# First feed forward: up and down slabs in turn, 14 of 16 down slabs by seven block products, sums on GpSimd

## The chip, the cores and the metric

One Trainium2 chip, one of its cores. The kernel is one launch that computes two transformer blocks for 256 tokens in float32. The metric is the device time of that launch in microseconds; three runs of the kernel before gave 883.88, 883.88 and 883.88, median 883.88. The profiled execution, from which all rows here come, took 884.08 with a span of 882.2.

## The reference, cut to what matters

The change touches the feed forward of the first block, with `h` 256 x 1024, `w1` 1024 x 4096 and `w2` 4096 x 1024:

```python
u = rmsnorm(h, norm_ff_g[l]) @ w1[l]
h = h + jnp.square(jax.nn.relu(u)) @ w2[l]
return rmsnorm(h, final_norm_g)
```

Before it stand the mixer and the cross attention, after it the second block, whose first weights are those of `in_w_in_2`.

## The kernel before, in words

**Slabs.** All weights stream through the core as numbered slabs of 128 partitions x 2048 float32 (1 MB). Three buffers in turn (`RING` = 3) hold the raw slab (`raw`) and its two parts: `whi`, the value rounded to fp32r, made by ScalarE's copy (`hi`, L1389), and `wlo`, the rest, made by VectorE's subtraction of two SBUF operands (`lo`, L1944). TensorE makes each product in three passes (`mm3`, L718 to L720): high by high, high by low, low by high. SyncE loads slab n when `lo` of slab n-3 is done; ScalarE splits slab n when it has landed and TensorE has finished slab n-3. Every engine has one queue in order, and the order of the work on each is written out by hand.

**An up slab** (16 of them, `w1`, 256 columns) gives two 128-row tiles of the hidden layer, transposed, by 48 matmuls of 256 columns (`t_slab`). ScalarE takes the relu from PSUM into `ru` (`relu_step`, L1695), VectorE squares it into `sq` (`square`, L2305), ScalarE rounds it into `hid_hi` (`relu_hi`, L1699), VectorE makes `hid_lo` (`square_lo`, L2319). All 32 hidden tiles are kept in SBUF.

**A down slab** (16 of them, `w2`, 256 rows) adds the product of two hidden tiles with 256 x 1024 weights to the four PSUM banks `acc`. Plainly this is 8 block products of three passes, 24 matmuls of 512 columns (`row_slab`). Six of the 16 (down slabs 1, 3, 5, 7, 9, 11) are done by the seven products of Winograd's form of Strassen's rule instead (`seven_slab`), 21 matmuls. Those need four sums of weight blocks and four of hidden blocks:

```python
link(dve.tensor_tensor(b22, b22, b12, ALU.subtract))
dve.tensor_tensor(b12, b12, b11, ALU.subtract).then_inc(sev["t"], 1)
...
link(dve.tensor_tensor(b11, b22, b11, ALU.add))
dve.tensor_tensor(b21, b21, b11, ALU.subtract).then_inc(sev["t"], 1)
```

All sums are VectorE's. The four weight sums (`forms`, 128 x 512 each) are made in place in the raw slab, then split by ScalarE (`forms_hi`, L1717) and VectorE (`forms_lo`, L2343) into the rooms of `xhi` and `xlo`, which are free once the last up slab is done. The four hidden sums (128 x 128 each) stand in `square`, three of them in room of `xn`. Such a slab is loaded by two DMAs of 512 KB, and only 1536 of its 2048 columns are split by `hi` and `lo`. Four of the seven products go to the banks `tb` and are added to `h` once, in `fold` (VectorE), after slab 11.

**Order.** All 16 up slabs run first (one by `first_slab`, which begins amid the transposes of `h`, 15 in a loop), then the 16 down slabs. The last one (`last_row_slab`) is followed by quarters of the residual (`residual`, VectorE) and their transposes. The second block begins there.

**GpSimd** has nothing in this stretch but `square_scale` and a DMA at its start, and `gain_fin` (L599) at its end.

Of the kernel before, what the change touches and what calls it, by code (L numbers as in the profile page):

```python
# [16 lines left out]
F32 = mybir.dt.float32  # L17
# [3 lines left out]
ALU = mybir.AluOpType  # L21
# [14 lines left out]
RING = 3  # L36
SLAB = 2048
# [9 lines left out]
def plan(w):  # L47
# [40 lines left out]
    cols("w1", w["w1"], 0, 16)  # L88
    rows("w2", w["w2"], 16)
# [20 lines left out]
def two_blocks(nc, w, out):  # L110
# [14 lines left out]
    SEVEN = [first["w2"] + j for j in (1, 3, 5, 7, 9, 11)]  # L125
# [5 lines left out]
    with ExitStack() as ctx:  # L131
# [63 lines left out]
        with ExitStack() as r3:  # L195
            hid_hi = sb("hid_hi", [P, FF1 // P, T], F32R, at=r3)
            hid_lo = sb("hid_lo", [P, FF1 // P, T], F32R, at=r3)
            ru = sb("ru", [P, 512], at=r3)
            sq = sb("sq", [P, 512], at=r3)
            sum_hi = sb("sum_hi", [P, len(SEVEN), 3 * P], F32R, at=r3)  # L200
            sum_lo = sb("sum_lo", [P, len(SEVEN), 3 * P], F32R, at=r3)
# [81 lines left out]
        sev = sems("sev", "t hi lo kept folded")  # L283
# [31 lines left out]
        lasts = [first["wo"] + 3, first["xo"] + 3, first["w2"] + 15, first["w3"] + 3, NS - 1]  # L315
# [3 lines left out]
        TURNED = {"h1": first["wo"] + 3, "h2": first["xo"] + 3, "x2": first["w2"] + 15}  # L319
# [116 lines left out]

        FORMS_HI, FORMS_LO = (room[:, 32:32 + SLAB].rearrange("p (s c) -> p s c", c=512) for room in (xhi_room, xlo_room))
        sums = xn[:, 0, 0:3 * P]

        def halves(t):  # L440

            return t[:, 0:4:3, :], t[:, 1:3, :]
# [11 lines left out]
        def _(sp):  # L454
            def load(n, src=None, wait=None):
# [3 lines left out]
                if n - RING in SEVEN:  # L459
                    sp.wait_ge(sev["lo"], 2 * SEVEN.index(n - RING) + 2)  # L460
# [54 lines left out]
            for n in range(RING + 1, first["w1"]):  # L515
# [17 lines left out]
        def _(pool):  # L533
# [120 lines left out]
            for m in range(1, LEVELS):  # L654
# [60 lines left out]
        def _(pe):  # L715
# [17 lines left out]
            def t_slab(n, hi, lo, bank, value=None, fresh=None):  # L733
# [4 lines left out]
                for c in range(slabs[n][3] // P):  # L738
                    o = tb[:, bank + c // 2, (c % 2) * T:(c % 2) * T + T]
# [35 lines left out]
            def seven_slab(j, hi, lo):  # L775

                n = first["w2"] + j
                i, k = SEVEN.index(n), 2 * j
                b_hi, b_lo = slab(whi, n, 2).rearrange("p k (s c) -> p (k s) c", c=512), \
                    low_slab(n, 2).rearrange("p k (s c) -> p (k s) c", c=512)  # L780
                first_one, last_one = i == 0, i == len(SEVEN) - 1

                def whole(kt, t):
                    return hi[:, kt, t * P:t * P + P], lo[:, kt, t * P:t * P + P]

                def summed(a):
# [409 lines left out]
            n0 = first["w1"] + 1  # L1196
            with pe.Fori(0, 5) as i:
                for u in range(RING):
                    pe.wait_ge(act_emptied, i * RING + (act_evacs[n0 + u] - RING))
                    t_slab(n0 + u, XHI["h2"], XLO["h2"], (u + 1) % RING, i * RING + (n0 + u + 1))  # L1200

            for j in range(15):
                pe.wait_ge(ffn["lo"], j + 1)
                if j == 1:
                    emptied(first["w1"] + 15)
                if first["w2"] + j in SEVEN:
                    seven_slab(j, hid_hi, hid_lo)
                else:
                    row_slab(first["w2"] + j, hid_hi, hid_lo, 2 * j, 32)
# [159 lines left out]
        def _(act):  # L1369
# [322 lines left out]
            def relu_step(bank, done, j, dst):  # L1692

                act.wait_ge(slab_done, done)
                act.activation(ru[:, :], tb[:, bank, :], ACT.Relu).then_inc(act_emptied, 1)  # L1695

            def relu_hi(j):
                act.wait_ge(ffn["sq"], j + 1)
                last = act.activation(hid_hi[:, 2 * j:2 * j + 2, :], sq[:, :], ACT.Copy)  # L1699
                if first["w2"] + j in SEVEN:  # L1700
                    last = act.activation(sum_hi[:, SEVEN.index(first["w2"] + j), :], sums, ACT.Copy)
                last.then_inc(ffn["hi"], 1)

            n0 = first["w1"]
            act.wait_ge(slab_done, n0 + 1)
            act.activation(ru[:, 0:T], tb[:, 0, 0:T], ACT.Relu)
            act.activation(ru[:, T:2 * T], acc[:, 1, 0, 0:T], ACT.Relu).then_inc(act_emptied, 1)
            hi(n0 + RING)
            relu_hi(0)
            def forms_hi(j):  # L1710

                n = first["w2"] + j
                i = SEVEN.index(n)
                act.wait_ge(slab_done, SEVEN[i - 1] + 1 if i else first["w2"])
                for half, (src, dst) in enumerate(zip(halves(raw_forms(n)), halves(FORMS_HI))):
                    act.wait_ge(sev["t"], 2 * i + half + 1)
                    act.activation(dst, src, ACT.Copy).then_inc(sev["hi"], 1)  # L1717

            for j in range(1, 16):
                relu_step(j % RING, n0 + j + 1, None, None)  # L1720
                if j == 15:
                    forms_hi(1)
                hi(n0 + j + RING)
                relu_hi(j)
            n0 = first["w2"]
            for j in range(14):
                if n0 + j + 2 in SEVEN:
                    forms_hi(j + 2)
                if n0 + j == SEVEN[-1]:
                    act.wait_ge(slab_done, n0 + j + 1)  # L1730
                    act.activation(ru[:, :], tb[:, 0, :], ACT.Copy).then_inc(sev["kept"], 1)
                hi(n0 + j + RING)
# [197 lines left out]
        def _(dve):  # L1930
# [372 lines left out]
            def square(j):  # L2303
                dve.wait_ge(act_emptied, act_evacs[first["w1"] + j])
                made = dve.tensor_tensor(sq[:, :], ru[:, :], ru[:, :], ALU.mult)  # L2305
                if first["w2"] + j in SEVEN:
                    link(made)
                    a11, a21, a12, a22 = (sq[:, i * P:i * P + P] for i in range(4))
                    s1, s2, s4 = (sums[:, i * P:i * P + P] for i in range(3))
                    link(dve.tensor_tensor(s1, a21, a22, ALU.add))  # L2310
                    link(dve.tensor_tensor(a21, a11, a21, ALU.subtract))
                    link(dve.tensor_tensor(s2, s1, a11, ALU.subtract))
                    made = dve.tensor_tensor(s4, a12, s2, ALU.subtract)
                made.then_inc(ffn["sq"], 1)

            def square_lo(j):
                dve.wait_ge(ffn["hi"], j + 1)
                dst, src = hid_lo[:, 2 * j:2 * j + 2, :], hid_hi[:, 2 * j:2 * j + 2, :]
                last = dve.tensor_tensor(dst, sq[:, :], src.bitcast(F32), ALU.subtract)  # L2319
# [45 lines left out]
            for j in range(16):  # L2365
                square(j)
                if j == 15:
                    forms_lo(1)
                lo(n0 + j + RING)
                square_lo(j)  # L2370
                if j == 14:
                    forms(1)
# [333 lines left out]
```

## Time and profile before

| | |
|---|---|
| median of three runs | 883.88 us |
| profiled execution | 884.08 us, span 882.2 us |
| TensorE matmuls | busy 874.6 us, 99% |
| VectorE | busy 647.6 us, 73% |
| ScalarE | busy 502.4 us, 57% |
| GpSimd | busy 117.9 us, 13% |
| granted TensorE clock | 1.0 of full speed |
| HBM read | 158.86 MB, 181 GB/s over the span |

Matmuls overlap in the pipeline, so their durations are longer than the distance from one start to the next; that distance is what a matmul costs. PE is TensorE's matmuls, DVE VectorE, ACT ScalarE, POOL GpSimd, SPq SyncE's DMA queue. A duration on DVE or POOL runs from the instruction's start in the record to its end and holds whatever it stood still in between.

### The profile page before, as it was taken

To read this page: it belongs to the slowest core of one execution; us is meant where nothing else is said; L and a number is where in the kernel's file an instruction comes from. 1 tells how busy PE (TensorE), PEld (TensorE's weight loads), DVE (VectorE), ACT (ScalarE), POOL (GpSimd) and SP (SyncE) were. 2 spreads that over 40 slices of the span, in tenths; PEclk is the share of its full clock that TensorE was granted. 3 is DMA by queue.
4 is the path that set the end of the run, shared out by engine and by line. 5 is a ranking of instruction groups with operands and counts; after the bars stand their busy time and mean duration, and the time that the engine had idled before them with its cause. 6 is when DMAs were issued, how large, how long until landed. Compare 5 with 4: busy or idle time off the path is not lost.

```text
span 882.2 us, 15673 instructions
## 1 busy us (share of the span) xinstructions
PE 874.6 (99%) x6269; PEld 809.7 (92%) x6269; DVE 647.6 (73%) x881; ACT 502.4 (57%) x741; POOL 117.9 (13%) x136
## 2 busy tenths in 40 slices
PE   9999999999999999999999999999999999999997
PEld 9998988989989999888899989999998899999886
DVE  5887987656538887998775548978686788888643
ACT  7786655546547555545473356656634766666432
POOL 5561433000001000000142250001000100000000
PEclk9999999999999999999999999999999999999999
DMA  9969444354535666466556554354556386676641
GB/s 304 319 226 311 164 144 144 104 177 148 172 94 187 195 195 197 160 230 219 191 184 210 191 191 141 104 188 138 174 191 191 105 225 195 194 198 201 192 143 48
DMA packets 137399, 160.67 MB, mean 182 GB/s; under 512 B 4161, under 2 KB 113857, under 8 KB 137089
## 3 DMA queue, kind: packets, MB, share of 16 engines
q1 hardware_dynamic: 135280, 152.83, 54.1%
q0 software_dynamic: 1344, 6.03, 2.0%
q10 hardware_dynamic: 720, 1.06, 0.3%
q8 instruction: 38, 0.62, 0.3%
q14 instruction: 17, 0.13, 0.1%
HBM read 158.86 MB, written 1.05 MB: 181 GB/s over the span
## 4 chain that ended last, share of the span: by engine, by line
PE 98%; issue 1%; ACT 0%; DVE 0%; POOL 0%; DVEq 0%; POOLq 0%; ACTq 0%
PE tb L718 18%; PE tb L719 18%; PE tb L720 18%; PE acc L718 11%; PE acc L720 11%; PE acc L719 11%; PE acc L1043 1%; PE tb L1242 0%; PE tb L1122 0%; PE acc L1272 0%; PE tb L1140 0%; PE acc L1140 0%; PE acc L1290 0%; PE acc L1122 0%; PE tb L1241 0%
## 5 line engine op out<-in xcount | busy, mean ns | idle before, releaser
L1944 DVE TENSOR_TENSOR wlo<-raw,whi 128x2048 fp32r<-128x2048 f32 (+1 forms) x138 | 313.9, 2279 | 118.5 <-ACT whi L1389 117.9
L1389 ACT ACTIVATE whi<-raw 128x2048 fp32r<-128x2048 f32 (+1 forms) x138 | 261.4, 1896 | 140.6 <-PE acc L720 85.2
L718 PE MATMUL tb<-xhi,whi 128*128 128x256 f32 x1192 | 331.8, 278 | 0.2
L719 PE MATMUL tb<-xlo,whi 128*128 128x256 f32 x1192 | 329.5, 276 | 0.0
L720 PE MATMUL tb<-xhi,wlo 128*128 128x256 f32 x1192 | 329.5, 276 | 0.0
L718 PEld LDWEIGHTS tb<-xhi,whi 128*128 128x128 f32 x1192 | 224.1, 188 | 1.1 <-issue 1.0
L719 PEld LDWEIGHTS tb<-xlo,whi 128*128 128x128 f32 x1192 | 224.2, 188 | 0.1
L720 PEld LDWEIGHTS tb<-xhi,wlo 128*128 128x128 f32 x1192 | 224.0, 188 | 0.0
L720 PE MATMUL acc<-whi,xlo 128*128 128x512 f32 x112 | 44.0, 393 | 0.0
L718 PE MATMUL acc<-whi,xhi 128*128 128x512 f32 x112 | 43.8, 392 | 0.0
L719 PE MATMUL acc<-wlo,xhi 128*128 128x512 f32 x112 | 43.8, 391 | 0.0
L1893 ACT ACTIVATE cy<-tb,cols 128x256 f32<-128x256 f32 x44 | 22.5, 561 | 32.3 <-PE tb L720 32.3
L711 POOL TENSOR_TENSOR rs<-rs,half_neg 128x1 f32<-128x1 f32 x6 | 3.3, 553 | 266.8 <-DVE rs L2563 266.8
L719 PE MATMUL acc<-wlo,vhi 128*128 128x512 f32 x88 | 34.2, 389 | 0.0
L718 PE MATMUL acc<-whi,vhi 128*128 128x512 f32 x88 | 34.2, 389 | 0.0
L720 PE MATMUL acc<-whi,vlo 128*128 128x512 f32 x88 | 34.2, 389 | 0.0
L718 PE MATMUL acc<-whi,hid_hi 128*128 128x512 f32 x86 | 33.6, 391 | 0.0
L720 PE MATMUL acc<-whi,hid_lo 128*128 128x512 f32 x86 | 33.5, 389 | 0.0
L719 PE MATMUL acc<-wlo,hid_hi 128*128 128x512 f32 x86 | 33.5, 389 | 0.0
L2619 DVE SCALAR_TENSOR_TENSOR cy<-tb,cols,cy 128x255 f32<-128x255 f32 x44 | 19.2, 478 | 14.1 <-ACT cy L1893 14.1
L718 PE MATMUL tb<-mhi,whi 128*128 128x256 f32 x96 | 27.1, 282 | 0.0
L720 PE MATMUL tb<-mhi,wlo 128*128 128x256 f32 x96 | 26.6, 277 | 0.0
(448 smaller groups left out, 1598.2 us busy)
## 6 DMA issues: line engine op xcount, KB each, us to landing
raw<-in_w_in SPq DMA_DIRECT2D x37, 1024.0 KB, 5.2
raw<-in_w SPq DMA_DIRECT2D x26, 1024.0 KB, 5.4
raw<-in_w_up SPq DMA_DIRECT2D x44, 512.0 KB, 5.0
raw<-in_w_down SPq DMA_DIRECT2D x22, 512.0 KB, 4.2
raw<-in_w_xkv SPq DMA_DIRECT2D x8, 1024.0 KB, 5.3
raw<-in_w_out SPq DMA_DIRECT2D x8, 1024.0 KB, 4.9
raw<-in_w SPq DMA_DIRECT2D x12, 512.0 KB, 4.5
raw<-in_w_mem_kv SPq DMA_DIRECT2D x4, 1024.0 KB, 5.2
```

The source lines that it names most:

```text
L711: pool.tensor_tensor(r, r, half_neg[:, 0:1], ALU.pow).then_inc(tail_rs, 1)
L718: pe.matmul(o, a_hi, b_hi, start=start, stop=False)
L719: pe.matmul(o, a_hi, b_lo, start=False, stop=False)
L720: return pe.matmul(o, a_lo, b_hi, start=False, stop=stop)
L1043: last = pe.matmul(acc[:, 1, t, i * 64:i * 64 + 64], a[:, s], lvl_view(b[:, s], m)[:, :, 1, :], start=True, stop=True)
L1389: act.activation(whi[:, n % RING, cut], raw[:, n % RING, cut], ACT.Copy).then_inc(hi_ready, 1)
L1893: last = act.activation(cy[:, b, g, :], tb[:, b, g * T:g * T + T], ACT.Identity, scale=cols[:, bass.ds(j + a, 1)], bias=cols[:, bass.ds(j ...
L1944: dve.tensor_tensor(low(n)[:, cut], raw[:, n % RING, cut], whi[:, n % RING, cut].bitcast(F32), ALU.subtract).then_inc(lo_ready, 1)
L2619: last = dve.scalar_tensor_tensor(cy[:, b, g, 1:], tb[:, b, g * T:g * T + T - 1], cols[:, bass.ds(j + c, 1)], cy[:, b, g, 1:], ALU.mult, A ...
```

## The change

The order of the slabs becomes up 0, up 1, down 0, up 2, down 1, ... up 15, down 14, down 15. Up slab j+1 lies between down slabs j-1 and j, so only three sets of hidden tiles are kept (`HIDS` = 3), and the room that this frees holds the weight sums and their parts in buffers of their own (`forms`, `forms_hi`, `forms_lo`, two each). Up products go to one bank, `acc[:, 1, 1, :]`. Down slabs 0 to 13 use the seven products; 14 and 15 are plain. All weight sums and hidden sums move from VectorE to GpSimd; the weight sums read the raw slab as it lands and write to `forms`. The four sums at the end of the seven products move to GpSimd as well, from one copy of the four `tb` banks (ScalarE, `kept`); VectorE's `fold` keeps four additions to `h`. The up loops become straight code on SyncE and TensorE.

```diff
-    cols("w1", w["w1"], 0, 16)
-    rows("w2", w["w2"], 16)
+    for kind, j in [("up", 0)] + [s for j in range(15) for s in (("up", j + 1), ("down", j))] + [("down", 15)]:
...
-    SEVEN = [first["w2"] + j for j in (1, 3, 5, 7, 9, 11)]
+    UP = [first["w1"] + max(2 * j - 1, 0) for j in range(16)]
+    DOWN = [first["w1"] + min(2 * j + 2, 31) for j in range(16)]
+    SEVEN = DOWN[:14]
...
# SyncE, load
                 if n - RING in SEVEN:
-                    sp.wait_ge(sev["lo"], 2 * SEVEN.index(n - RING) + 2)
+                    sp.wait_ge(sev["t"], 2 * SEVEN.index(n - RING) + 2)
...
# GpSimd
+            def weight_sums(j):
+                i, n = j, DOWN[j]
+                b12, b11, b21, b22 = (raw_forms(n)[:, s, :] for s in range(4))
+                t3, t1, t2, t4 = (forms[:, i % 2, s, :] for s in range(4))
+                pool.wait_ge(raw_landed[n % RING], landed[n])
+                if i >= 2:
+                    pool.wait_ge(sev["lo"], 2 * i - 2)
+                pool.tensor_tensor(t3, b22, b12, ALU.subtract)
+                pool.tensor_tensor(t1, b12, b11, ALU.subtract).then_inc(sev["t"], 1)
+                pool.wait_ge(sev["t"], 2 * i + 1)
+                link(pool.tensor_tensor(t2, t3, b11, ALU.add))
+                pool.tensor_tensor(t4, b21, t2, ALU.subtract).then_inc(sev["t"], 1)
+            def hidden_sums(j):
+                a11, a21, a12, a22, s1, s2, s4 = (sq[:, s * P:s * P + P] for s in range(7))
+                pool.wait_ge(ffn["sq"], j + 1)
+                link(pool.tensor_tensor(s1, a21, a22, ALU.add))
+                pool.tensor_tensor(a21, a11, a21, ALU.subtract)
+                link(pool.tensor_tensor(s2, s1, a11, ALU.subtract))
+                pool.tensor_tensor(s4, a12, s2, ALU.subtract).then_inc(sev["sums"], 1)
+            pool.wait_ge(slab_done, first["w1"])
+            weight_sums(0)
             square_scale()
...
+            for j in range(len(SEVEN)):
+                if j:
+                    weight_sums(j)
+                hidden_sums(j)
+            pool.wait_ge(sev["kept"], 1)
+            link(pool.tensor_tensor(q11, q00, q11, ALU.add))
+            link(pool.tensor_tensor(q10, q11, q10, ALU.add))
+            link(pool.tensor_tensor(q11, q11, q01, ALU.add))
+            pool.tensor_tensor(q01, q10, q01, ALU.add).then_inc(sev["sums"], 1)
             gain_fin()
...
# TensorE
             for j in range(15):
+                emptied(UP[j] if j else first["xo"] + 3)
+                t_slab(UP[j + 1], XHI["h2"], XLO["h2"], None, whole=acc[:, 1, 1, :])
+                if j == 0:
+                    emptied(UP[0])
                 pe.wait_ge(ffn["lo"], j + 1)
+                if DOWN[j] in SEVEN:
+                    seven_slab(j)
                 else:
+                    plain_slab(j)
             pe.wait_ge(ffn["lo"], 16)
-            pe.wait_ge(sev["folded"], 1)
-            last_row_slab("x2", hid_hi, hid_lo, 30)
+            pe.wait_ge(sev["kept"], 1)
+            last_row_slab("x2", hidden(hid_hi, 15), hidden(hid_lo, 15), 0)
# in seven_slab: three products of split weights, then
+                pe.wait_ge(sev["lo"], 2 * j + 1)
+                mm3(tb[:, 1, :], *part(S1), *form(T1), first_one, last_one)
+                mm3(tb[:, 3, :], *part(S3), *form(T3), first_one, last_one)
+                pe.wait_ge(sev["lo"], 2 * j + 2)
+                mm3(tb[:, 2, :], *part(S2), *form(T2), first_one, last_one)
+                mm3(acc[:, 0, 1, :], *part(A22), *form(T4), first_one, False).then_inc(slab_done, 1)
...
# ScalarE
+            def relu(j):
+                act.wait_ge(slab_done, UP[j] + 1)
+                if j:
+                    act.wait_ge(ffn["sq"], j)
+                    act.activation(ru[:, :], acc[:, 1, 1, :], ACT.Relu).then_inc(act_emptied, 1)
...
+            form_hi(0, 0)
+            form_hi(0, 1)
+            relu(0)
+            hi(n0 + 3)
+            hidden_hi(0)
+            for j in range(15):
+                if j:
+                    hi(n0 + 2 * j + 3)
+                if DOWN[j + 1] in SEVEN:
+                    form_hi(j + 1, 0)
+                    form_hi(j + 1, 1)
+                elif DOWN[j] not in SEVEN:
+                    act.wait_ge(slab_done, SEVEN[-1] + 1)
+                    act.activation(forms[:, 0, :, :], tb[:, :, :], ACT.Copy).then_inc(sev["kept"], 1)
+                relu(j + 1)
+                hi(n0 + 2 * j + 4)
+                hidden_hi(j + 1)
...
# VectorE
+            square(0)
+            form_lo(0, 0)
+            form_lo(0, 1)
+            lo(n0 + 3)
+            hidden_lo(0)
+            for j in range(15):
+                seven = DOWN[j + 1] in SEVEN
+                if j:
+                    lo(n0 + 2 * j + 3)
+                if seven:
+                    form_lo(j + 1, 0)
+                square(j + 1)
+                if seven:
+                    form_lo(j + 1, 1)
+                lo(n0 + 2 * j + 4)
+                hidden_lo(j + 1)
+            fold()
             residual("x2", C["norm_mix_pre_2"], rs[:, NORM["h2"], :])
```

`form_hi` waits for the first or the second pair of weight sums (`sev["t"]`), `hidden_hi` for the hidden sums (`sev["sums"]`), `form_lo` and `hidden_lo` for ScalarE's copies. `hidden_hi` and `hidden_lo` are 896 wide (four hidden blocks and three sums), `form_hi` and `form_lo` 1024 wide.

## Rows read from the trace of the kernel before

**Rows 1.** The page: busy time by engine (first part), chain that ended last (fourth).

```profile
PE 874.6 (99%) x6269; PEld 809.7 (92%) x6269; DVE 647.6 (73%) x881; ACT 502.4 (57%) x741; POOL 117.9 (13%) x136
...
PE 98%; issue 1%; ACT 0%; DVE 0%; POOL 0%; DVEq 0%; POOLq 0%; ACTq 0%
```

**Rows 2.** Busy time by stretch: bounds, us, engines, granted clock, DMA share, GB/s; six down slabs.

```profile
356.00:382.00 26.00, 26.00 (x120) 21.66 (x119) 24.37 (x25) 15.77 (x13) 0.00 (x0) 1.00 0.46 162
```

**Rows 3.** Timeline of PE: start us, duration us, engine, line; second up slab, last down slab.

```profile
274.99 0.29 PE L718 MATMUL tb<-xhi,whi 128*128 128x256 f32 x1
...
279.93 0.28 PE L719 MATMUL tb<-xlo,whi 128*128 128x256 f32 x1
...
280.95 0.28 PE L719 MATMUL tb<-xlo,whi 128*128 128x256 f32 x1
...
434.19 0.39 PE L718 MATMUL acc<-whi,hid_hi 128*128 128x512 f32 x1
...
436.46 0.39 PE L719 MATMUL acc<-wlo,hid_hi 128*128 128x512 f32 x1
```

**Rows 4.** Groups by line and shape, 270 to 445 us: count, busy us, mean ns, idle before.

```profile
L1944 DVE TENSOR_TENSOR wlo<-raw,whi 128x2048 fp32r<-128x2048 f32 x27 | 61.6, 2288 | 13.6 <-ACT whi L1389 13.5
...
L2343 DVE TENSOR_TENSOR xlo<-raw,xhi 128x1024 fp32r<-128x1024 f32 x12 | 14.5, 1221 | 0.0
L1717 ACT ACTIVATE xhi<-raw 128x1024 fp32r<-128x1024 f32 x12 | 12.7, 1062 | 19.6 <-DVE raw L2332 17.6 <-DVE raw L2335 2.0
L2305 DVE TENSOR_TENSOR sq<-ru 128x512 f32<-128x512 f32 x16 | 11.1, 692 | 7.0 <-ACT ru L1695 6.6 <-ACT ru L1707 0.4
L2319 DVE TENSOR_TENSOR hid_lo<-sq,hid_hi 128x512 fp32r<-128x512 f32 x16 | 10.9, 683 | 0.0
L1944 DVE TENSOR_TENSOR wlo<-raw,whi 128x1536 fp32r<-128x1536 f32 x6 | 10.5, 1757 | 1.3 <-ACT whi L1389 1.2
...
L1695 ACT ACTIVATE ru<-tb 128x512 f32<-128x512 f32 x15 | 9.0, 601 | 30.9 <-PE tb L720 30.9
```

**Rows 5.** Groups by line and shape on POOL, whole span.

```profile
L599 POOL TENSOR_TENSOR xn<-h,xn 128x512 f32<-128x512 f32 x4 | 5.1, 1285 | 158.0 <-DVE h L1984 158.0
...
L697 POOL TENSOR_TENSOR upad<-uw,upad 128x256 f32<-128x256 f32 x4 | 3.0, 744 | 0.3
...
L691 POOL TENSOR_TENSOR uw<-upad 128x256 f32<-128x256 f32 x4 | 2.5, 614 | 33.5 <-DVE upad L2394 33.2
...
L554 POOL TENSOR_TENSOR small<-small,ident 128x8 f32<-128x8 f32 x1 | 0.2, 203 | 0.1
```

**Rows 6.** Timeline of DVE and POOL where `lo` meets sums on GpSimd.

```profile
504.20 2.43 DVE L1944 TENSOR_TENSOR wlo<-raw,whi 128x2048 fp32r<-128x2048 f32 x1 [2.61 <-ACT whi L1389]
...
504.56 2.54 POOL L691 TENSOR_TENSOR uw<-uw 128x256 f32<-128x256 f32 x1
```

**Rows 7.** Timeline of POOL and DVE, 29 to 37 us.

```profile
29.87 4.53 POOL L631 TENSOR_TENSOR qs<-qs,fs 128x512 f32<-128x512 f32 x2
...
33.16 3.38 DVE L1944 TENSOR_TENSOR wlo<-raw,whi 128x2048 fp32r<-128x2048 f32 x1
```

**Rows 8.** Timeline of POOL and DVE, 436 to 438 us; `acc` is in PSUM.

```profile
436.76 2.54 POOL L599 TENSOR_TENSOR xn<-h,xn 128x512 f32<-128x512 f32 x2 [156.85 <-DVE h L1984]
...
437.12 0.75 DVE L1984 SCALAR_TENSOR_TENSOR h<-acc,rs,h 128x512 f32<-128x512 f32 x1 [0.52 <-PE acc L720]
```

**Rows 9.** Timeline of DVE and ACT at the start of the feed forward.

```profile
272.50 4.48 DVE L1944 TENSOR_TENSOR wlo<-raw,whi 128x2048 fp32r<-128x2048 f32 x2
...
276.71 0.37 ACT L1706 ACTIVATE ru<-tb 128x256 f32<-128x256 f32 x1
```

**Rows 10.** DMA issues, 270 to 445 us: count, KB each, median us to landing.

```profile
raw<-in_w SPq DMA_DIRECT2D x22, 1024.0 KB, 5.4
```

**Rows 11.** Timeline of PE, 7 us after the span's start.

```profile
7.27 0.41 PE L718 MATMUL tb<-xhi,whi 128*128 128x256 f32 x1
7.49 0.39 PE L719 MATMUL tb<-xlo,whi 128*128 128x256 f32 x1
```

More of the change, by code:

```diff
@@ L282, in two_blocks @@
         ffn = sems("ffn", "sq hi lo")
-        sev = sems("sev", "t hi lo kept folded")
+        sev = sems("sev", "sums t hi lo kept")
         pl = sems("pl", "ready mm hi lo")
@@ L435, in two_blocks, with hidden, hid_width @@
         turned_x = turned_mem = xn[:, :, :].rearrange("p t c -> p (t c)").rearrange("p (k m) -> p k m", k=KT)
[L437 to L442, printed above, removed]
+        def hidden(room, j):
+            return room[:, j % HIDS, 0:512].rearrange("p (k t) -> p k t", k=2)
+        def hid_width(j):
+            return 7 * P if DOWN[j] in SEVEN else 4 * P
         def raw_forms(n):
@@ L514, in _ @@
                 sp.dma_start(fpt[:, 0, 64 * i:64 * i + 64], w[n].broadcast_to([P, 64])).then_inc(lam_in, 16)
-            for n in range(RING + 1, first["w1"]):
+            for n in range(RING + 1, first["cv"]):
                 if n in PIECES:
@@ L731, in emptied, with t_slab @@
                     pe.wait_ge(dve_emptied, dve_evacs[n])
-            def t_slab(n, hi, lo, bank, value=None, fresh=None):
+            def t_slab(n, hi, lo, bank, value=None, fresh=None, whole=None):
                 split_ready(n, value)
@@ L738, in t_slab @@
                 for c in range(slabs[n][3] // P):
-                    o = tb[:, bank + c // 2, (c % 2) * T:(c % 2) * T + T]
+                    o = (tb[:, bank + c // 2, :] if whole is None else whole)[:, (c % 2) * T:(c % 2) * T + T]
                     for k in range(nk):
@@ new lines, in seven_slab, with plain_slab @@
+                mm3(acc[:, 0, 1, :], *part(A22), *form(T4), first_one, False).then_inc(slab_done, 1)
+            def plain_slab(j):
+                n, hi, lo = DOWN[j], hidden(hid_hi, j), hidden(hid_lo, j)
+                split_ready(n)
+                b_hi, b_lo = slab(whi, n, 2), low_slab(n, 2)
+                for t in range(TT):
+                    for c in range(2):
+                        if t * c:
+                            emptied(UP[15])
+                        for k in range(2):
+                            a, w = slice(t * P, t * P + P), slice(c * 512, c * 512 + 512)
+                            last = mm3(acc[:, c, t, :], hi[:, k, a], lo[:, k, a], b_hi[:, k, w], b_lo[:, k, w],
+                                       t * c == 1 and k == 0, False)
+                last.then_inc(slab_done, 1)
@@ L1689, in _ @@
             sumsq("h2", h)
[L1692 to L1702, printed above, removed]
@@ L1704, in _ @@
-            n0 = first["w1"]
[L1705 to L1732, printed above, removed]
+            def relu(j):
[3 more added lines that the diff above has]
+                    act.activation(ru[:, :], acc[:, 1, 1, :], ACT.Relu).then_inc(act_emptied, 1)
+                else:
+                    act.activation(ru[:, 0:T], tb[:, 0, 0:T], ACT.Relu)
+                    act.activation(ru[:, T:2 * T], acc[:, 1, 0, 0:T], ACT.Relu).then_inc(act_emptied, 1)
@@ new lines, in hidden_hi, with form_hi @@
+            def hidden_hi(j):
+                if DOWN[j] in SEVEN:
+                    act.wait_ge(sev["sums"], j + 1)
+                else:
+                    act.wait_ge(ffn["sq"], j + 1)
+                w = hid_width(j)
+                act.activation(hid_hi[:, j % HIDS, 0:w], sq[:, 0:w], ACT.Copy).then_inc(ffn["hi"], 1)
+            def form_hi(j, half):
+                s, b = slice(2 * half, 2 * half + 2), j % 2
+                act.wait_ge(sev["t"], 2 * j + half + 1)
+                act.activation(forms_hi[:, b, s, :], forms[:, b, s, :], ACT.Copy).then_inc(sev["hi"], 1)
@@ L2303, in square @@
             def square(j):
[L2304 to L2313, printed above, removed]
@@ L2326, in forms @@
-            def forms(j):
-                b12, b11, b21, b22 = (raw_forms(first["w2"] + j)[:, i, :] for i in range(4))
-                i = SEVEN.index(first["w2"] + j)
-                dve.wait_ge(lo_ready, first["w2"] + j + 1)
-                link(dve.tensor_tensor(b22, b22, b12, ALU.subtract))
-                dve.tensor_tensor(b12, b12, b11, ALU.subtract).then_inc(sev["t"], 1)
-                dve.wait_ge(sev["t"], 2 * i + 1)
-                link(dve.tensor_tensor(b11, b22, b11, ALU.add))
-                dve.tensor_tensor(b21, b21, b11, ALU.subtract).then_inc(sev["t"], 1)
@@ L2337, in forms_lo @@
-            def forms_lo(j):
-                n = first["w2"] + j
-                i = SEVEN.index(n)
-                for half, (src, high, dst) in enumerate(zip(halves(raw_forms(n)), halves(FORMS_HI), halves(FORMS_LO))):
-                    dve.wait_ge(sev["hi"], 2 * i + half + 1)
-                    dve.tensor_tensor(dst, src, high.bitcast(F32), ALU.subtract).then_inc(sev["lo"], 1)
+                dve.wait_ge(act_emptied, act_evacs[UP[j]])
+                dve.tensor_tensor(sq[:, 0:512], ru[:, :], ru[:, :], ALU.mult).then_inc(ffn["sq"], 1)
@@ new lines, in hidden_lo, with form_lo @@
+            def hidden_lo(j):
+                dve.wait_ge(ffn["hi"], j + 1)
+                w = hid_width(j)
+                dve.tensor_tensor(hid_lo[:, j % HIDS, 0:w], sq[:, 0:w], hid_hi[:, j % HIDS, 0:w].bitcast(F32),
+                                  ALU.subtract).then_inc(ffn["lo"], 1)
+                dve.wait_ge(ffn["lo"], j + 1)
+            def form_lo(j, half):
+                s, b = slice(2 * half, 2 * half + 2), j % 2
+                dve.wait_ge(sev["hi"], 2 * j + half + 1)
+                dve.tensor_tensor(forms_lo[:, b, s, :], forms[:, b, s, :], forms_hi[:, b, s, :].bitcast(F32),
+                                  ALU.subtract).then_inc(sev["lo"], 1)
@@ L2364, in _ @@
-            n0 = first["w1"]
[L2365 to L2372, printed above, removed]
-            n0 = first["w2"]
-            dve.wait_ge(nrm["rs"], RS["h2"] + 2)
-            for j in range(14):
-                if n0 + j + 2 in SEVEN:
-                    forms_lo(j + 2)
-                if n0 + j == SEVEN[-1]:
-                    fold()
-                lo(n0 + j + RING)
-                if n0 + j + RING in SEVEN:
-                    forms(j + RING)
@@ L2384, in _ @@
-            dve.wait_ge(sev["folded"], 1)
-            dve.wait_ge(nrm["rs"], RS["h2"] + 2)
+                    last = dve.scalar_tensor_tensor(hq, forms[:, 0, s, :], r[:, t:t + 1], hq, ALU.mult, ALU.add)
+                link(last)
+            n0 = first["w1"]
+            square(0)
[14 more added lines that the diff above has]
+                hidden_lo(j + 1)
```

99 lines of the change are left out of this document (36 added, 63 removed).

## The prediction

> **What bounds the kernel now.** I read the page's busy times and chain first, then busy time by stretch, the timeline of PE, the groups by line inside the feed forward, and last every place where GpSimd works while VectorE does. PE is busy 99% of the span and carries 98% of the chain [rows 1]: the kernel is a stream of matmuls, and a change gains only by fewer matmuls or loses by making PE wait. A matmul costs the distance between starts. For 256 columns that is (280.95 - 279.93)/9 = 0.1133 us, for 512 columns (436.46 - 434.19)/10 = 0.227 us [rows 3]. So an up slab is 48 x 0.1133 = 5.44 us, a plain down slab 24 x 0.227 = 5.44, a seven slab 21 x 0.227 = 4.76. From the second up slab to the last down slab PE takes 434.19 - 274.99 = 159.2 us [rows 3]; 15 x 5.44 + 9 x 5.44 + 6 x 4.76 = 159.1, so nothing is lost there. VectorE is nearly full where the sevens run: 24.37 of 26 us, GpSimd at 0.00 [rows 2].
>
> **What the change can gain.** Eight more sevens save 8 x 3 x 0.227 = 5.4 us. A pair (up and seven) is 5.44 + 4.76 = 10.2 us of PE.
>
> **What it costs: one pair's work on VectorE and GpSimd.** VectorE per pair: `lo` of the up slab 2.288, `lo` of the seven 1.757, two `form_lo` of 1.221, `square` 0.692 [rows 4], and `hidden_lo`, 896 wide, between 0.683 (512) and 1.221 (1024) [rows 4], by interpolation 1.09. Sum 8.27 us. GpSimd per pair: four weight sums of 512. An undisturbed 512 product takes 1.285 [rows 5]; a subtraction of 256 took 0.744 where an addition took 0.614 [rows 5], so a 512 subtraction may take 1.285 x 0.744/0.614 = 1.56. I take 1.33, nearest to the row of the same width; 4 x 1.33 = 5.32 (ends 5.1 and 6.0). Four hidden sums of 128: between 0.203 (8 wide) and 0.614 (256 wide) [rows 5], I take half of the latter, 0.31; 1.24 (ends 0.8 and 2.5). Four waits on its own result at about 0.1: 0.4 (L554 and its neighbours stand 0.1 us idle between such steps [rows 5]). Sum 6.96 us.
>
> Each sum alone fits under 10.2. The question is whether they run side by side. The trace says no. At 504.56 an addition of 256 on GpSimd, 0.614 when alone [rows 5], takes 2.54: it ends at 507.10, 0.47 after `lo` ends at 504.20 + 2.43 = 506.63 [rows 6]. It stood still for the whole of `lo`, and got through its 0.61 from 0.14 before `lo`'s recorded end. The other way round, `lo` at 33.16 takes 3.38 against 2.288: GpSimd's second product ends at 29.87 + 4.53 = 34.40, and `lo` ends at 36.54, 2.14 later [rows 7], again 0.15 short of a full `lo`. Where VectorE reads one operand from PSUM they don't meet: the residual's 0.75 and GpSimd's two products in 2.54 (1.27 each) overlap at no cost [rows 8]. In the changed stretch all six VectorE instructions of a pair read two SBUF operands, and all eight of GpSimd read SBUF. I take it that the two engines exclude each other there, instruction by instruction, and that each handover saves 0.13 us of the recorded durations.
>
> The Trainium skill says the same in SBUF — State Buffer, section Who interferes with whom: a VectorE instruction with two SBUF inputs and a GpSimd instruction that reads SBUF share a port, and the loser blocks until the other's whole instruction is over. Held to the recorded ends, without the 0.13 us, this rule would make each period below 17.1 us and the time about 977 us; rows 6 and 7 speak for the shorter hold.
>
> **The period.** One part of a pair leaves the port empty. `relu(j+1)` stands on ScalarE behind `form_hi(j+1)`, which waits for the second pair of weight sums; these stand on GpSimd behind `hidden_sums(j)`. While `form_hi` (1.062) and the relu (0.601) [rows 4] run, VectorE waits at `square(j+1)`, which needs the relu, and GpSimd at `hidden_sums(j+1)`, which needs the square. With three handovers of some 0.06 us that is 1.84 us with nobody at the port. Everything else of the pair stands between two relus: `square`, `form_lo`, `lo`, hidden sums, weight sums, `hidden_lo`, `lo`, `form_lo`. Ten of the passages go from one engine to the other: 10 x 0.13 = 1.3. Period: 8.27 + 6.96 + 1.84 - 1.3 = 15.8 us, against 10.2 of PE. PE idles about 5.5 us of each period: once before the up product (it needs the relu to free its one bank) and once before the seven (it needs `hidden_lo`).
>
> **The sum, on the profiled execution.** Start: GpSimd begins the first sums when slab `w1` 0 may start, about 268.9, some 5.7 us of work, and meets two `lo` (272.50, 4.48 us for both [rows 9]); so they end about 277 to 278. ScalarE is done with the squares of `h` at 276.71 [rows 9]; two `form_hi` of 1.06 [rows 4] and the relu in two halves of 0.37 [rows 9] then end about 280. Up slab 1 needs none of that and runs from 274.99 as now. One period later, at 295.8, the relu that up slab 2 waits for is done. Twelve more periods to up slab 14: 295.8 + 12 x 15.75 = 484.8. From there up 14 (5.44), 1.4 until hidden 13 is split (from the relu: square 0.69, `form_lo` 1.22, `lo` 1.76, sums 1.4, ScalarE 0.95, `hidden_lo` 1.09, less 0.3 of handovers and the 5.44), seven 13 (4.76), up 15 and plain 14 (5.44 each), and about 2.1 until hidden tile 15 is split, for its relu stands behind ScalarE's copy of four banks: 24.6, so the last slab begins at 509.4 instead of 434.19, 75.2 later. GpSimd's four end sums lie beside the last slabs, but `fold`, 4 x 0.75 [rows 8], stands ahead of the first residual on VectorE, which could begin 1.4 us into the last slab: 3.0 - 1.4 = 1.6. Sum: 884.08 + 75.2 + 1.6 = 960.9 of the profiled time; the median stands 0.2 below it, so 960.7, and I predict 960.
>
> **Costed at nothing.** The weight loads: 2 MB per period at 5.4 us from issue to landing [rows 10]; each load is released by a `lo` about 10 us before it is used, and the wait on `sev["t"]` in place of `sev["lo"]` frees the raw slab earlier; SyncE holds nothing else in this stretch. If that cover went, a load late by 1 us would cost up to 14 us in all. `square_scale` and the gain's DMA move behind the first sums; what they make is used only in `fold` and `gain_fin`, 200 us later. The straight code instead of loops: other slabs are straight code already, with PE at 99% [rows 1]. `hidden_hi`, 896 wide on ScalarE (1.06 for 1024 at most [rows 4]) lies beside GpSimd's next weight sum. The final additions gain nothing on PE, since `last_row_slab` no longer waits for `fold`, but PE never idled there.
>
> **Rivals.** First, not slower: no exclusion in these forms, that is, GpSimd's subtractions and VectorE's run side by side as in [rows 8]. Then the loop relu 0.60, square 0.69, hidden sums 1.4, weight sums 5.5, `form_hi` 1.06 and handovers 0.4 takes 9.7, under PE's 10.2, and PE sets the period; from a 512 sum of 1.46 us on it doesn't. The gain of 5.4 is met at the start: hidden tile 0 waits on VectorE behind two `form_lo` and a `lo` and is ready at about 280 + 0.7 + 2.4 + 2.3 + 1.1 = 286.5, PE stands from 280.4, 6 us. With 0 to 1.6 at the end: 884 to 886. For it: rows 8. Against: rows 6 and 7, where the very instruction `lo` is blocked and blocks. Second, exclusion with the empty part filled or a much shorter hold: a period of 15.2 - 1.3 = 13.9 or less, down to 11, which is 13 x 1.8 = 24 to 13 x 4.7 = 62 less: 898 to 937. Against it: the order on all three queues is fixed, and in it nothing can use the gap. Third, the clock falls. It was 1.00 with PE never idle [rows 2]; here PE idles a third of each period. At the start of the kernel, after PE had been idle, matmuls of 256 columns stood 7.49 - 7.27 = 0.22 us apart [rows 11], twice the 0.1133, which is the lower of the two levels (1.2 and 2.4 GHz). A pair at that level all the time is 20.4 us, and the time 960 + 13 x 4.7 = 1021; against it, such a PE would be busy without a break. The Trainium skill, TensorE: Matmul & The Clock Gate, Part 1: The HAM clock gate, has the clock fall after idle time and rise with sustained work; by it the clock could fall in some periods, and the time would be between the two. Fourth, the change is not what it says: the sums are not made "at the landing" but behind the previous hidden sums; that is in the forecast.
>
> **How the numbers follow.** Forecast (period 15 to 17.7: 935 to 995) 0.78; shorter hold 0.08; clock 0.07, half of it above 995; no exclusion 0.07. Faster or slower counts from 0.2% on, 1.8 us, about what a measurement can tell from no change: no exclusion gives faster 0.02, same 0.04, slower 0.01. Together faster 0.02, same 0.04, slower 0.94. The range: 925 to 995, which holds the forecast and the upper part of the shorter hold.
>
> **What would show it.** Right: up slabs start 15 to 17 us apart; in the stretch of the feed forward GpSimd's 512 sums last well over 1.33 us on average and VectorE's `lo` well over 2.29; PE's idle time there is about 75 us, before the up matmuls ended by ScalarE's relu and before the sevens by VectorE's `hidden_lo`. Wrong: `lo` at 2.29 beside sums at 1.3 (no exclusion); matmuls of 512 columns 0.45 us apart (clock); waits for `raw` (loads).

## The result, and the profile after

The changed kernel takes 955.26 us (four runs, 955.21 to 955.68) against 883.88 before: ratio 1.0809, interval 1.079 to 1.0827, 71.4 us slower. The profiled execution has a span of 953.5 us.

The page of the changed kernel, busy time by engine, two of the rows of 40 slices, and the chain that ended last:

```profile
PE 894.1 (94%) x6245; PEld 822.2 (86%) x6245; DVE 662.5 (69%) x839; ACT 517.1 (54%) x751; POOL 298.4 (31%) x252
...
POOL 5642342000067878787843407000100000000000
PEclk9999999999998799998999999999999999999999
...
PE 75%; POOL 18%; issue 3%; DVE 2%; ACT 2%; POOLq 0%; DVEq 0%; ACTq 0%
```

GpSimd's busy time rises from 117.9 to 298.4 us [rows 1], and 18% of the chain, about 172 us, is GpSimd's: in every pair of the feed forward the chain now runs through its sums, 12.8 us of each period (the rest is mostly the square and the relu). One period of it in the timeline (start us, duration us, engine, line), by engine:

```profile
371.42 0.69 DVE L2364 TENSOR_TENSOR sq<-ru 128x512 f32<-128x512 f32 x1 [2.73 <-ACT ru L1752]
372.03 1.22 DVE L2378 TENSOR_TENSOR forms_lo<-forms,forms_hi 128x1024 fp32r<-128x1024 f32 x1
373.16 2.01 DVE L2002 TENSOR_TENSOR wlo<-raw,whi 128x1536 fp32r<-128x1536 f32 x1
377.47 1.18 DVE L2370 TENSOR_TENSOR hid_lo<-sq,hid_hi 128x896 fp32r<-128x896 f32 x1 [2.29 <-ACT hid_hi L1764]
379.35 2.60 DVE L2002 TENSOR_TENSOR wlo<-raw,whi 128x2048 fp32r<-128x2048 f32 x1 [0.70 <-ACT whi L1444]
381.87 2.31 DVE L2378 TENSOR_TENSOR forms_lo<-forms,forms_hi 128x1024 fp32r<-128x1024 f32 x1
386.91 0.69 DVE L2364 TENSOR_TENSOR sq<-ru 128x512 f32<-128x512 f32 x1 [2.73 <-ACT ru L1752]
...
372.19 1.37 POOL L688 TENSOR_TENSOR sq<-sq 128x128 f32<-128x128 f32 x1 [2.38 <-DVE sq L2364]
373.64 1.85 POOL L689 TENSOR_TENSOR sq<-sq 128x128 f32<-128x128 f32 x1
375.46 0.45 POOL L690 TENSOR_TENSOR sq<-sq 128x128 f32<-128x128 f32 x1
375.99 0.46 POOL L691 TENSOR_TENSOR sq<-sq 128x128 f32<-128x128 f32 x1
376.41 1.29 POOL L678 TENSOR_TENSOR forms<-raw 128x512 f32<-128x512 f32 x1
377.66 2.15 POOL L679 TENSOR_TENSOR forms<-raw 128x512 f32<-128x512 f32 x1
379.88 3.22 POOL L681 TENSOR_TENSOR forms<-forms,raw 128x512 f32<-128x512 f32 x1
383.18 2.12 POOL L682 TENSOR_TENSOR forms<-raw,forms 128x512 f32<-128x512 f32 x1
...
385.34 1.06 ACT L1770 ACTIVATE forms_hi<-forms 128x1024 fp32r<-128x1024 f32 x1 [4.44 <-POOL forms L682]
386.30 0.58 ACT L1752 ACTIVATE ru<-acc 128x512 f32<-128x512 f32 x1
```

Square to square is 386.91 - 371.42 = 15.49 us; all periods from the second pair to the fourteenth are 15.5 within 0.02. Undisturbed, a hidden sum (`sq`) takes 0.45 us and a weight sum (`forms`) 1.29. The others are longer by the time in which VectorE has the way: L681 starts at 379.88 while `lo` runs until 379.35 + 2.60 = 381.95, and ends 1.15 later, at 383.10; `form_lo`, from 381.87, in turn waits for L681 and ends 1.08 after it, at 384.18. And from 385.30, where the last sum ends, to 386.91 neither engine works: ScalarE makes `form_hi`, then the relu.

The same by line and shape, over the stretch 268 to 510 us (count, busy us, mean ns). In the kernel before the means were 1221 ns for `form_lo`, 2288 for `lo` and 1285 for a GpSimd product of 512 columns [rows 4, 5]:

```profile
L2378 DVE TENSOR_TENSOR forms_lo<-forms,forms_hi 128x1024 fp32r<-128x1024 f32 x28 | 47.4, 1695 | 2.3 <-ACT forms_hi L1770 2.3
L2002 DVE TENSOR_TENSOR wlo<-raw,whi 128x2048 fp32r<-128x2048 f32 x18 | 45.9, 2549 | 10.3 <-ACT whi L1444 10.3
L681 POOL TENSOR_TENSOR forms<-forms,raw 128x512 f32<-128x512 f32 x14 | 41.2, 2943 | 1.1
...
L682 POOL TENSOR_TENSOR forms<-raw,forms 128x512 f32<-128x512 f32 x14 | 30.9, 2205 | 1.1
...
L678 POOL TENSOR_TENSOR forms<-raw 128x512 f32<-128x512 f32 x14 | 18.1, 1293 | 51.5 <-PE acc L763 51.5
```

TensorE in the timeline: the first seven, an up slab, a seven, the up slab 14, the last down slab, with the idle time and its releaser in brackets:

```profile
287.72 0.76 PE L761 MATMUL tb<-whi,hid_hi 128*128 128x512 f32 x1 [6.96 <-issue]
...
309.48 0.38 PE L761 MATMUL acc<-xhi,whi 128*128 128x256 f32 x1 [3.17 <-ACT ru L1752]
...
363.22 0.50 PE L761 MATMUL tb<-whi,hid_hi 128*128 128x512 f32 x1 [1.49 <-DVE hid_lo L2370]
...
479.89 0.39 PE L761 MATMUL acc<-xhi,whi 128*128 128x256 f32 x1 [3.12 <-ACT ru L1752]
...
504.67 0.50 PE L761 MATMUL acc<-whi,hid_hi 128*128 128x512 f32 x1 [1.61 <-DVE hid_lo L2370]
```

It waits 3.2 us before nearly every up slab for the relu (37.1 us in all), 7.0 before the first seven, and up to 1.55 before five of the later ones for `hidden_lo` (5.2 in all). The last slab begins at 504.67 instead of 434.19 [rows 3], 70.5 us later: that is nearly all of the result.

### The profile page after: what moved, and what is told of

Read it like the earlier page. It is cut to its first block, busy times and chain, and to the rows that moved or that the text cites. A ratio compares the mean times of both kernels' runs of the same rounds, so it can differ in the third digit from the quotient of the medians.

```text
span 953.5 us, 15649 instructions
## 1 busy us (share of the span) xinstructions
PE 894.1 (94%) x6245; PEld 822.2 (86%) x6245; DVE 662.5 (69%) x839; ACT 517.1 (54%) x751; POOL 298.4 (31%) x252
## 4 chain that ended last, share of the span: by engine, by line
PE 75%; POOL 18%; issue 3%; DVE 2%; ACT 2%; POOLq 0%; DVEq 0%; ACTq 0%
PE tb L761 13%; PE tb L763 13%; PE tb L762 13%; PE acc L761 9%; PE acc L763 9%; PE acc L762 9%; POOL forms L681 4%; POOL forms L682 3%; POOL forms L679 3%; POOL sq L689 2%; POOL sq L688 2%; POOL forms L678 2%; PE acc L1102 1%; DVE sq L2364 1%; ACT ru L1752 1%
## 5 line engine op out<-in xcount | busy, mean ns | idle before, releaser
L761 PE MATMUL tb<-xhi,whi 128*128 128x256 f32 x952 | 265.3, 279 | 0.5 <-issue 0.3
L763 PE MATMUL tb<-xhi,wlo 128*128 128x256 f32 x952 | 263.0, 276 | 0.0
L762 PE MATMUL tb<-xlo,whi 128*128 128x256 f32 x952 | 263.0, 276 | 0.0
L761 PE MATMUL acc<-xhi,whi 128*128 128x256 f32 x304 | 93.0, 306 | 37.1 <-ACT ru L1752 37.1
L761 PEld LDWEIGHTS acc<-xhi,whi 128*128 128x128 f32 x304 | 64.3, 212 | 42.2 <-ACT ru L1752 42.1
L762 PE MATMUL acc<-xlo,whi 128*128 128x256 f32 x304 | 91.1, 300 | 0.0
L763 PE MATMUL acc<-xhi,wlo 128*128 128x256 f32 x304 | 90.9, 299 | 0.0
L762 PEld LDWEIGHTS acc<-xlo,whi 128*128 128x128 f32 x304 | 64.3, 211 | 0.1
L763 PEld LDWEIGHTS acc<-xhi,wlo 128*128 128x128 f32 x304 | 64.2, 211 | 0.0
L2378 DVE TENSOR_TENSOR forms_lo<-forms,forms_hi 128x1024 fp32r<-128x1024 f32 x28 | 47.4, 1695 | 2.3 <-ACT forms_hi L1770 2.3
L681 POOL TENSOR_TENSOR forms<-forms,raw 128x512 f32<-128x512 f32 x14 | 41.2, 2943 | 1.1
```

Of the source, the lines that this page charges most:

```text
L681: link(pool.tensor_tensor(t2, t3, b11, ALU.add))
L761: pe.matmul(o, a_hi, b_hi, start=start, stop=False)
L762: pe.matmul(o, a_hi, b_lo, start=False, stop=False)
L763: return pe.matmul(o, a_lo, b_hi, start=False, stop=stop)
L2378: dve.tensor_tensor(forms_lo[:, b, s, :], forms[:, b, s, :], forms_hi[:, b, s, :].bitcast(F32), ALU.subtract).then_inc(sev["lo"], 1)
```

## The experiments

Three theories. A: an instruction of VectorE with two SBUF operands and one of GpSimd that reads SBUF exclude each other, so their times add up to a period. B: GpSimd's sums are simply slow and the others wait for them. C: the interleaved order, or the clock that falls in PE's waits, costs the time, whoever sums. Times are medians; the kernel before had a median of 883.75 beside the first four and 884.01 beside the last three.

**Sums on VectorE.** The bodies of `weight_sums` and `hidden_sums` moved, and called there:

```diff
# GpSimd
-            weight_sums(0)
...
-            for j in range(len(SEVEN)):
-                if j:
-                    weight_sums(j)
-                hidden_sums(j)
...
# VectorE, in weight_sums
+                dve.tensor_tensor(t3, b22, b12, ALU.subtract)
+                dve.tensor_tensor(t1, b12, b11, ALU.subtract).then_inc(sev["t"], 1)
...
# VectorE, in the loop
                 square(j + 1)
                 if seven:
+                    hidden_sums(j + 1)
                     form_lo(j + 1, 1)
                 lo(n0 + 2 * j + 4)
                 hidden_lo(j + 1)
+                weight_sums(j + 2)
```

> All weight and hidden sums on VectorE, same order of slabs, same buffers, same waits; GpSimd keeps only the four end sums. Theory A (a VectorE instruction with two SBUF operands and a GpSimd instruction that reads SBUF exclude each other, so their times add up): VectorE has 8.27 us of its own plus 4 x 0.69 and 4 x 0.29 of sums, 12.2 us per pair, so a period of 12.2 to 12.5 us and 908 to 918 us: 40 us faster than the change, still 30 slower than before. Rival B (GpSimd's sums are simply slow on their own, and the others wait for them): shorter sums, VectorE's queue is then the bound; also 908 to 918, so this run doesn't part A from B. Rival C (the interleaved order itself, or the granted clock falling in PE's waits, costs the time, whoever sums): 945 us or more.

908.66 us, ratio 1.0281 (1.0264 to 1.0298). The same arithmetic on the engine that was said to be full is 46.6 us faster than on the idle one. Busy time between 300 and 430 us (bounds, us, PE, PEld, DVE, ACT, POOL, clock):

```profile
300.00:430.00 130.00, 120.61 (x779) 106.09 (x779) 127.35 (x155) 74.03 (x67) 0.00 (x0) 1.00 0.54 178
```

VectorE is the bound, 127.35 of 130; the squares stand 11.83 us apart, a little under the 12.2 of the sum since instructions in a row overlap. The first half of C falls: the order of the slabs is that of the change, and 46.6 of the 71.4 us are gone. Its second half, the clock, isn't tested here, since PE's waits are down to about 1.0 us per period and the granted clock stays at 1.00.

**Relu first.** One move on ScalarE, for the pairs that are followed by a seven:

```diff
                     form_hi(j + 1, 0)
+                    relu(j + 1)
                     form_hi(j + 1, 1)
...
-                relu(j + 1)
+                if DOWN[j + 1] not in SEVEN:
+                    relu(j + 1)
```

> The change with one move on ScalarE: relu(j+1) stands between the two form_hi of slab j+1 instead of behind both. Theory A: the 1.8 us of each period in which neither VectorE nor GpSimd has anything to do is filled, and the period becomes the sum of both engines' instructions, 8.27 + 6.96 - 1.3 = 13.9, at least 13.5: 928 to 935 us. Rival B: with the relu out of the loop through the weight sums GpSimd alone needs under 7 us per pair, PE's 10.2 sets the period: 884 to 890 us. Rival C: no change, 950 us or more.

935.91 us, 1.0596 (1.0578 to 1.0613), just above A's 928 to 935. The squares are 14.0 us apart instead of 15.49, where A said 13.9:

```profile
361.22 1.77 DVE L2366 TENSOR_TENSOR sq<-ru 128x512 f32<-128x512 f32 x1
...
375.22 1.77 DVE L2366 TENSOR_TENSOR sq<-ru 128x512 f32<-128x512 f32 x1
```

B's 884 to 890 are far off: with the relu out of the loop nothing of GpSimd's own length explains 14.0.

**Narrow sums.** GpSimd's sums on 8 columns; the other columns stay as they are, set to zero once at the start.

```diff
-                b12, b11, b21, b22 = (raw_forms(n)[:, s, :] for s in range(4))
-                t3, t1, t2, t4 = (forms[:, i % 2, s, :] for s in range(4))
+                b12, b11, b21, b22 = (raw_forms(n)[:, s, 0:8] for s in range(4))
+                t3, t1, t2, t4 = (forms[:, i % 2, s, 0:8] for s in range(4))
...
# hidden_sums
-                a11, a21, a12, a22, s1, s2, s4 = (sq[:, s * P:s * P + P] for s in range(7))
+                a11, a21, a12, a22, s1, s2, s4 = (sq[:, s * P:s * P + 8] for s in range(7))
...
+            pool.memset(forms[:, :, :, :], 0.0)
+            link(pool.memset(sq[:, 512:896], 0.0))
```

> GpSimd's sums cut to 8 columns each; the other columns are left out (they stay as they were), every wait stays. Theory A: eight instructions of 0.2 us instead of 7 us per pair leave VectorE's 8.27 + some 1.6, about PE's 10.2: period 10.2 to 10.7, 884 to 893 us. Rival B: the same, 884 to 893. Rival C: the order and the clock are as they were: 930 us or more.

890.44 us, 1.0077 (1.006 to 1.0094). The period is PE's, 10.25; the granted clock from 300 to 430 us is 1.00 and PE is busy 130.00 of 130. By line, 268 to 510 us:

```profile
L2004 DVE TENSOR_TENSOR wlo<-raw,whi 128x2048 fp32r<-128x2048 f32 x30 | 69.1, 2310 | 32.8 <-ACT whi L1446 32.8
...
L689 POOL TENSOR_TENSOR sq<-sq 128x8 f32<-128x8 f32 x14 | 21.8, 1558 | 1.1
```

GpSimd still stands behind VectorE (1.56 us for a sum that takes 0.20), but costs VectorE nothing any more: `lo` is at 2.31.

**Write only.** Each sum replaced by an iota of the same shape into the same place, which leaves the sums out:

```diff
-                pool.tensor_tensor(t3, b22, b12, ALU.subtract)
...
+                def fill(t):
+                    return pool.iota(t, [[1, t.shape[-1]]], base=0, channel_multiplier=0,
+                                     allow_small_or_imprecise_dtypes=True)
+                fill(t3)
...
```

> Each of GpSimd's sums is replaced by an iota of the same shape into the same place, which writes and reads nothing (the sums are left out); every wait stays. An iota of 128 columns takes 0.22 to 0.26 us in the trace of before, so one of 512 about 0.6 to 1.0. Theory A, if only reads exclude: VectorE never stands still, period 10.2, 884 to 890 us. Theory A, if writes exclude too: 8.27 + 4 x 0.8 + 4 x 0.24 + 0.4 + 1.84 - 1.3 = 13.4 us, about 925 us. Rival B: loop of 7 to 8 us, 884 to 890. Rival C: 930 us or more.

889.33 us, 1.0064 (1.0048 to 1.0081), period 10.25. By line:

```profile
L2008 DVE TENSOR_TENSOR wlo<-raw,whi 128x2048 fp32r<-128x2048 f32 x31 | 71.6, 2314 | 49.2 <-ACT whi L1450 49.2
...
L2384 DVE TENSOR_TENSOR forms_lo<-forms,forms_hi 128x1024 fp32r<-128x1024 f32 x28 | 34.1, 1219 | 0.0
L679 POOL IOTA forms<- 128x512 f32 x56 | 30.7, 561 | 72.3 <-PE acc L769 51.4 <-DMA raw<-in_w 19.0
```

Only a GpSimd instruction that reads holds VectorE up: `form_lo` is back at 1219 ns while GpSimd writes as many columns as in the change. An iota of 512 takes 0.56 us, less than half a sum, so by itself this run says little against B; the pair at the end of this section does.

**Hidden sums on VectorE, weight sums on GpSimd.**

```diff
# GpSimd
-                hidden_sums(j)
...
# VectorE, in the loop
                 square(j + 1)
                 if seven:
+                    hidden_sums(j + 1)
                     form_lo(j + 1, 1)
```

> The change with only the four hidden sums of a pair moved back to VectorE; the weight sums stay on GpSimd. Theory A: GpSimd's 1.64 us of hidden sums are replaced by 4 x 0.29 on VectorE and fewer handovers save less; period about 15.1 instead of 15.5, 940 to 950 us. Rival B (GpSimd's own length sets the loop): 886 to 895 us, since the loop relu, square, sums, form_hi without exclusion is about 9 us.

936.63 us, 1.0595 (1.0577 to 1.0612): 18.6 us faster than the change, 3 us below the lower end of A's figure. The periods alternate, 15.2 and 13.2 us:

```profile
362.67 0.68 DVE L2354 TENSOR_TENSOR sq<-ru 128x512 f32<-128x512 f32 x1
...
377.85 0.69 DVE L2354 TENSOR_TENSOR sq<-ru 128x512 f32<-128x512 f32 x1 [2.75 <-ACT ru L1742]
...
391.05 0.68 DVE L2354 TENSOR_TENSOR sq<-ru 128x512 f32<-128x512 f32 x1
```

What A's figure left out: GpSimd's weight sums no longer stand behind hidden sums but begin as soon as the slab lands. In the longer period that is 4.2 us after the square, and the time in which neither engine works, 1.61 us, is there as in the change; in the shorter one they begin 0.1 us after the square, are over early, and that empty time is gone.

**Sums that nobody waits for, in the kernel before**, and the same with a write only. From the start of the feed forward, in the order of before, on a buffer of their own:

```diff
+            pool.wait_ge(slab_done, first["w1"] + 1)
+            link(pool.memset(spare[:, :, :], 0.0))
+            for _ in range(48):
+                link(pool.tensor_tensor(spare[:, 1, :], spare[:, 0, :], spare[:, 0, :], ALU.subtract))
# and in the other run
+                link(pool.iota(spare[:, 1, :], [[1, 448]], base=0, channel_multiplier=0,
+                               allow_small_or_imprecise_dtypes=True))
```

> The kernel before, with 48 subtractions of 448 columns on GpSimd from the start of the feed forward on, of a buffer that nobody else reads or writes and for which nobody waits. Theory A: each takes the way from VectorE for about 1.0 us; 48 us are added to VectorE's work, of which the idle 18% of some ten slabs, 9 to 15 us, absorb a part: 905 to 925 us, and lo in that stretch lasts well over 2.3 us. Rival B and C: nobody waits for GpSimd and the order is that of before: 883 to 885 us.

> As the run with 48 subtractions in the kernel before, but each is an iota of 448 columns into the same buffer, which reads nothing. Theory A with only reads excluding: 883 to 885 us, lo at 2.29. Theory A with writes excluding too: 48 x 0.6 = 29 us on VectorE, half of it absorbed: 890 to 905 us. Rivals B and C: 883 to 885.

With reads 903.91 us, 1.0219 (1.0202 to 1.0236), 20 us slower, just under the forecast range; with writes 883.88, 0.9999 (0.999 to 1.0009). By line, 276 to 380 us, first with reads, then with writes:

```profile
L672 POOL TENSOR_TENSOR spare<-spare 128x448 f32<-128x448 f32 x48 | 70.7, 1472 | 3.8
...
L1949 DVE TENSOR_TENSOR wlo<-raw,whi 128x2048 fp32r<-128x2048 f32 x15 | 37.2, 2478 | 1.1 <-ACT whi L1394 1.1
...
L2310 DVE TENSOR_TENSOR sq<-ru 128x512 f32<-128x512 f32 x16 | 16.6, 1037 | 1.4 <-ACT ru L1700 0.6 <-ACT ru L1712 0.4
```

```profile
L1950 DVE TENSOR_TENSOR wlo<-raw,whi 128x2048 fp32r<-128x2048 f32 x17 | 38.9, 2289 | 8.5 <-ACT whi L1395 8.4
...
L672 POOL IOTA spare<- 128x448 f32 x48 | 24.3, 507 | 3.3
L2311 DVE TENSOR_TENSOR sq<-ru 128x512 f32<-128x512 f32 x16 | 11.1, 692 | 7.0 <-ACT ru L1701 6.5 <-ACT ru L1713 0.4
```

Work for which no semaphore waits slows the kernel by 20 us if it reads, and by nothing if it writes; the square goes from 692 to 1037 ns. B has nothing to say to that, and the order in C neither. The Trainium skill, SBUF — State Buffer, section Who interferes with whom, says just this of a VectorE instruction with two SBUF inputs: it contends with a GpSimd instruction that reads SBUF, not with one that only writes it. The ratios 1.0219 and 0.9999 agree. In the run with reads the chain goes through VectorE from 284 to 353 us.

None of these beats the kernel before; even with sums that cost nothing (narrow, write only) it is 5 to 7 us behind, for the reason below.

## Why the prediction was right, point by point

960 was forecast, within 925 to 995; 955.26 came.

**The exclusion** is shown, by the pair of runs with idle work and by the durations in the period. The hold is shorter than the recorded durations, as read from rows 6 and 7: L681 ends 1.15 us after `lo`, 0.14 short of its 1.29. The period has nine such handovers (ten in the forecast); together they save 1.3 us, as forecast.

**The period** was put at 15.8 and is 15.49. Its terms, though, were off and cancel: a subtraction of 512 takes 1.293 (1.33 taken; the 1.56 that the ratio of two rows of 256 gave doesn't occur), four hidden sums 4 x 0.45 = 1.8 instead of 1.24, since 128 columns cost more than half of 256. With both changed the terms give 8.27 + 5.16 + 1.8 + 0.4 + 1.61 = 17.24, so 1.75 goes off instead of 1.3. The difference is not in the handovers: three of the four waits on GpSimd's own results lie under an instruction of VectorE (0.3 of the 0.4), and instructions in a row on one engine overlap a little. That the sum came within 0.3 us is in part luck.

**The empty part** was put at 1.84: it is 386.91 - 385.30 = 1.61. Relu first closes it and gives back 19.3 us, about 1.5 per period.

**The start**: relu 0 ends at 278.9 (280 said), the relu of up slab 1 at 293.9 (295.8). **The end**: 504.67 - 479.89 = 24.8 us from up slab 14 to the last slab (24.6), though made up otherwise: up slab 14 runs slow, 7.2 us, and the wait of 1.4 for hidden 13 is gone. In all 70.5 instead of 75.2: the start is 1.9 us shorter, the twelve periods 3.0, the end 0.2 longer. **`fold`** holds up the residual: the first transposes of `h` begin 3.57 us into the last slab instead of 2.73, 0.84 later (1.6 said). First before, then after:

```profile
436.92 0.60 PE L856 MATMUL tb<-ident,h 128*128 128x128 f32 x4
```

```profile
508.24 0.66 PE L915 MATMUL tb<-ident,h 128*128 128x128 f32 x4 [0.55 <-DVE h L2042]
```

**PE's idle time** was to be about 75 us. From 274.99 to 504.67 it is 50.9. At full speed the matmuls of this stretch would take 15 x 5.44 + 14 x 4.76 + 5.44 = 153.7 of its 229.7 us and leave 76; about 25 us of that went into slower matmuls, see the clock.

**No gain without exclusion** was forecast as a rival, 884 to 886, for the first seven waits while VectorE works through two `form_lo` and a `lo`. With sums that cost nothing it is 889 to 890: the wait before the first seven is there, 4.45 us (write only) and 6.2 (narrow). The rival left out the wait of 1.6 us before the last slab, and that the matmuls of the first seven are slow after its wait. Write only, from its first matmul to the first of the next up slab:

```profile
285.10 0.77 PE L767 MATMUL tb<-whi,hid_hi 128*128 128x512 f32 x1 [4.45 <-ACT ru L1758]
...
289.07 0.63 PE L767 MATMUL tb<-forms_hi,hid_hi 128*128 128x512 f32 x1
289.50 0.63 PE L768 MATMUL tb<-forms_lo,hid_hi 128*128 128x512 f32 x1
...
292.56 0.28 PE L767 MATMUL acc<-xhi,whi 128*128 128x256 f32 x1
```

That slab takes 292.56 - 285.10 = 7.46 us instead of 4.76, its matmuls 0.43 apart at first instead of 0.227; narrow 6.7 us. The granted clock is 0.50 from 285 to 290 us. With 4.45 + 2.7 + 1.6, 0.05 for each of 13 periods and 0.84 at `fold`, less the gain of 5.4, the sum is 4.8 of the 5.1 us between the two spans (887.3 and 882.2).

**The clock.** As a rival I let a falling clock cost time. It fell: granted clock by stretch (after PE, PEld, DVE, ACT and POOL) is 0.84 and 0.96 where it was 1.00 [rows 2],

```profile
300.00:330.00 30.00, 23.24 (x121) 20.58 (x120) 19.57 (x12) 12.51 (x12) 24.62 (x17) 0.84 0.40 135
...
360.00:400.00 40.00, 29.89 (x175) 25.82 (x173) 25.56 (x15) 17.29 (x15) 34.38 (x23) 0.96 0.43 141
```

and part of an up slab runs at the lower of the two levels (1.2 and 2.4 GHz), 0.21 us from start to start as in rows 11, after 3.2 us of waiting:

```profile
310.92 0.41 PE L761 MATMUL acc<-xhi,whi 128*128 128x256 f32 x1
311.13 0.41 PE L762 MATMUL acc<-xlo,whi 128*128 128x256 f32 x1
```

But the periods at 0.84 and at 0.96 are equally long: PE needs about 10.2 of 15.5 us at full speed, and slower matmuls take from its waits. So in the periods of the change that step of the rival failed: the fall comes, its price doesn't. The Trainium skill, TensorE: Matmul & The Clock Gate, Part 1: The HAM clock gate, has the clock fall after idle time; the trace agrees. The price does come where PE is the bound: the 2.7 us behind the first wait of write only.

## What to carry to other kernels

Before work goes from VectorE to GpSimd, ask of both sides whether they read SBUF and with how many operands: the times of VectorE's instructions with two SBUF operands and of GpSimd's sums that read SBUF add up, and a sum that costs VectorE 0.69 us costs the pair 1.29. That one operand from PSUM avoids this rests on rows 8 alone; no run here varies it. Look for the bound in the sum of both engines' times per period, not in either one's busy share. Where TensorE is the bound, a wait can cost more than its length: one of 4.45 us cost another 2.7 here. And where an order is written out by hand, look for what stands idle on both while a third engine finishes: here moving the relu ahead of one `form_hi` gives back 19 us.

## What the runs showed of the hardware that was not expected

A GpSimd sum of 8 columns, 0.20 us alone, may stand for 1.56 us behind VectorE without VectorE losing anything (`lo` 2310 against 2288 ns): what hurts VectorE is the other's length, not its presence. A GpSimd sum of 128 columns takes 0.45 us, one of 512 1.29, addition and subtraction alike; an iota of 512, which reads nothing, 0.56.
